# Turning the memory tiles in pairs between mixing units, and filling the last cross head from two output units instead of four

## What is computed

```python
x = x + merged @ w_mix_out[l]
x = x + cross_attention(rms_norm(x, xattn_norm_g[l]), rms_norm(mem, mem_norm_g[l]),
                        w_xq[l], w_xkv[l], w_xo[l])
x = x + swiglu(rms_norm(x, ffn_norm_g[l]), w_ffn_gate[l], w_ffn_up[l], w_ffn_down[l])
```

## Time and profile before

| | |
|---|---|
| device time, median of 3 runs | 2035.38 us (2035.09 to 2038.58) |
| device time of the profiled execution | 2037.93 us |
| its span, first to last instruction | 2036.1 us |
| mean granted clock of PE | 0.989 of full |
| PE busy | 1944.5 us, 95% |
| DVE, ACT, POOL busy | 1075.8, 496.6, 1240.7 us |
| DMA | 177.39 MB, 87 GB/s in the mean |

### The profile page before, as it was taken

One profiled execution on the slowest core, in us unless ns is written; L12 is line 12 of the kernel. 1 busy time (PEld: TensorE's weight loads), 2 busy tenths in 40 slices (PEclk: granted clock), 3 DMA queues, 4 the chain that ended last, 5 costly groups with the idle time before them and its releaser, 6 DMA issues.

```text
span 2036.1 us, 23483 instructions
## 1 busy us (share of the span) xinstructions
PE 1944.5 (95%) x9015; PEld 1594.0 (78%) x9015; DVE 1075.8 (53%) x1514; ACT 496.6 (24%) x998; POOL 1240.7 (61%) x1018
## 2 busy tenths in 40 slices
PE   8888887999999999999999999999999989999997
PEld 6666666888888888888888778888779878888886
DVE  5677758998364131227866675333655563223134
ACT  4444443432122010012233333100222221001012
POOL 6333326878766776676633444776667587676662
PEclk9999998999999999999999999999999999999999
DMA  5221102333333333333312322333433233333321
GB/s 161 72 60 56 53 25 78 99 107 104 95 94 96 101 93 94 102 94 94 92 46 59 78 63 69 98 93 88 124 94 105 72 104 95 102 94 95 102 78 57
DMA packets 341169, 177.39 MB, mean 87 GB/s; under 512 B 14453, under 2 KB 338203, under 8 KB 341060
## 3 DMA queue, kind: packets, MB, share of 16 engines
q1 hardware_dynamic: 338834, 173.14, 29.5%
q10 hardware_dynamic: 2226, 2.76, 0.6%
HBM read 173.75 MB, written 2.13 MB: 86 GB/s over the span
## 4 chain that ended last, share of the span: by engine, by line
PE 75%; DVE 18%; issue 3%; ACT 3%; POOL 0%; ACTq 0%; DMA 0%; SPq 0%; DVEq 0%; POOLq 0%
PE bank L650 22%; PE bank L654 22%; PE bank L652 22%; PE bank L772 2%; PE bank L749 1%; DVE aPR L1710 1%; DVE aPR L1712 1%; DVE IT L1818 1%; DVE XC L1799 1%; DVE HS L1828 1%; DVE HS L1829 1%; DVE aPR L1702 1%; PE bank L738 1%; PE bank L718 1%; DVE ACC L1823 1%
## 5 line engine op out<-in xcount | busy, mean ns | idle before, releaser
L615 POOL TENSOR_TENSOR WL<-RAW,WH 128x1024 fp32r<-128x1024 f32 (+3 forms) x331 | 812.9, 2456 | 27.5
L650 PE MATMUL bank<-HH,WH 128*128 128x512 f32 x1560 | 622.7, 399 | 14.6 <-DVE SQ L1670 7.4
L654 PE MATMUL bank<-HH,WL 128*128 128x512 f32 x1560 | 617.1, 396 | 0.0
L652 PE MATMUL bank<-HL,WH 128*128 128x512 f32 x1560 | 614.3, 394 | 0.0
L611 POOL TENSOR_TENSOR gate<-gate 128x1 f32<-128x1 f32 x331 | 89.2, 270 | 737.8 <-PE bank L654 687.9
L650 PEld LDWEIGHTS bank<-HH,WH 128*128 128x128 f32 x1560 | 295.3, 189 | 79.0 <-issue 20.6
L612 POOL TENSOR_SCALAR WH<-RAW 128x1024 fp32r<-128x1024 f32 (+3 forms) x331 | 344.6, 1041 | 0.0
L652 PEld LDWEIGHTS bank<-HL,WH 128*128 128x128 f32 x1560 | 295.4, 189 | 60.1 <-issue 4.2
L654 PEld LDWEIGHTS bank<-HH,WL 128*128 128x128 f32 x1560 | 294.7, 189 | 60.4 <-issue 1.9
L1869 DVE TENSOR_TENSOR X<-X,bank 128x512 f32<-128x512 f32 x80 | 54.9, 687 | 202.7 <-PE bank L654 202.7
L650 PE MATMUL bank<-UH,WH 128*128 128x512 f32 x256 | 99.9, 390 | 0.3
(11 more groups left out here) (407 smaller groups left out, 3205.0 us busy)
## 6 DMA issues: line engine op xcount, KB each, us to landing
RAW<-in_w_in SPq DMA_DIRECT2D x107, 512.0 KB, 3.7
RAW<-in_w_up SPq DMA_DIRECT2D x32, 512.0 KB, 3.9
RAW<-in_w_down SPq DMA_DIRECT2D x32, 512.0 KB, 3.9
RAW<-in_w_ffn_gate SPq DMA_DIRECT2D x22, 512.0 KB, 3.7
RAW<-in_w_ffn_up SPq DMA_DIRECT2D x22, 512.0 KB, 3.7
RAW<-in_w_xkv SPq DMA_DIRECT2D x16, 512.0 KB, 3.8
RAW<-in_w_ffn_down SPq DMA_DIRECT2D x16, 512.0 KB, 3.5
RAW<-in_w_proj_attn SPq DMA_DIRECT2D x8, 512.0 KB, 3.8
```

The lines of the kernel that those rows point to most:

```text
L615: nc.gpsimd.tensor_tensor(WL[:, s, 0:k, :], RAW[:, s, 0:k, :], WH[:, s, 0:k, :].bitcast(F32), ALU.subtract).then_inc(S_[f"unit_cut{s}"], 1)
L650: mm(psum[s][:, 0:n], WH[:, s, k, :], hi(k), start=(k == 0), stop=False)
L652: mm(psum[s][:, 0:n], WH[:, s, k, :], lo(k), start=False, stop=False)
L654: last = mm(psum[s][:, 0:n], WL[:, s, k, :], hi(k), start=False, stop=(k == tiles - 1))
```

## The change

It rewrites where the pairs of transposes stand: tiles 2e−8 and 2e−7 both behind unit e, for e from 4 to 7; nothing stands inside a unit or in the queries. `mem_after` is changed to match, so that ACT and DVE handle the same two tiles behind the norm chunk of unit e. In the last cross head the fronts are those of two output units, 36 matmuls instead of 72; the fills are 4, 4, 4, 12 and 6, 6 instead of 6, 6, 6, 18 and 10, 12, so 36 instead of 58 issue inside the head, and none of the fronts behind it. Units 2 and 3 of the output then run whole behind the tails of units 0 and 1.

```diff
--- before.py
+++ after.py
@@ -408,7 +408,7 @@
 
         def mem_after(e):
 
-            return {4: [0], 5: [1, 2], 6: [3, 4], 7: [5, 6, 7]}.get(e, [])
+            return [] if e < 4 else [2 * e - 8, 2 * e - 7]
 
         KIND1, KIND_FOX, KIND_SWA = Causal(1), Causal(2), Window(2)
         block = top.enter_context(nc.Block())
@@ -1007,18 +1007,11 @@
                 last.then_inc(S_["mem_t"], 1)
 
             for e in range(DC):
-                rows = from_pair("out2", e // 4, e % 4, MGC, cut_pair("mgc_hi", "mgc_lo") if e == 0 else None)
-                if e >= 5:
-                    run(rows, 12)
-                    mem_transposed(2 * e - 9)
-                run(rows)
-                if e >= 4:
-                    mem_transposed(2 * e - 8)
-
-            queries0 = from_h("cross", 0, 0, cut_of("n4"))
-            run(queries0, 12)
-            mem_transposed(DC - 1)
-            run(queries0)
+                run(from_pair("out2", e // 4, e % 4, MGC, cut_pair("mgc_hi", "mgc_lo") if e == 0 else None))
+                for m in mem_after(e):
+                    mem_transposed(m)
+
+            run(from_h("cross", 0, 0, cut_of("n4")))
             norm_stat("n4", "n3")
             pe.wait_ge(S_["mem_acc"], DC + 1)
             mm(OUTB[:, 0:MEM], ones[:], ACCM[:], start=True, stop=True).then_inc(once("mem_stat")[0], 1)
@@ -1088,7 +1081,7 @@
                 cross(h, ahead, (8, 8, 8, 24), (16, 16))
                 run(ahead)
 
-            fronts = [from_pair("xout", 0, e, XO, cut_pair("x_out_hi", "x_out_lo", 2)) for e in range(4)]
+            fronts = [from_pair("xout", 0, e, XO, cut_pair("x_out_hi", "x_out_lo", 2)) for e in range(2)]
 
             def front_rows():
                 for rows in fronts:
@@ -1097,12 +1090,12 @@
                         yield
 
             ahead = front_rows()
-            cross(3, ahead, (6, 6, 6, 18), (10, 12))
+            cross(3, ahead, (4, 4, 4, 12), (6, 6))
             run(ahead)
             for rows in fronts:
                 run(rows)
-            for e in range(4, DC):
-                run(from_pair("xout", 1, e % 4, XO))
+            for e in range(2, DC):
+                run(from_pair("xout", e // 4, e % 4, XO))
 
 
             def ffn_group(name, g, first=False):
```

## The result

The changed kernel takes 2022.92 us in the median of 4 runs (2022.19 to 2023.13); the kernel before, with the run made beside it, 2036.98 (4 runs, 2035.09 to 2041.70). The ratio is 0.9924, with a 95% interval of 0.9906 to 0.9943: faster, by 12 to 19 us. The forecast was 2018.0, with a range from 2016.5 in its own case up to 2024. The range holds the result; the forecast itself is 4.9 us too low.

A forecast was written before the change was run, and what follows sets the result against it. TensorE, busy 95% of the span, was taken as the bound, so only its waits and low-clock work counted. Savings of 10.7 and 6.7 us, 17.4 off the 2035.38 median, gave 2018.0; range 2016.5 to 2024.

The forecast's parts named there:

- its own case: Whole kernel, forecast 2018.0, chance 0.52; fewer waits in the edited stages give 2016.5, run spread up to 2019.5.
- Part 1: Mixing units 4 to 7 and queries: transposes in double pairs take 25.90 us to the statistics against 36.59, −10.7 us.
- The breakdown by terms: Mixing stage's saving: some 7.6 us gaps, 4.9 low clock, 0.5 turns, with 2.5 given back.
- The port's rival: Mixing: POOL's WL starts ahead of tile 1's sum, later pairs wait, queries end 2.1 us later: 2020.1; chance 0.18.
- Part 2: Last cross head and output units: two fronts finish product 0 earlier, DVE's norm no longer binds, −6.7 us.
- (a): Last cross head, before the turns: PE waits 0.47 us for the last probabilities; bounds none and 1.8 us.
- The bound "none": Before the last head's turns: no wait if a DVE scaling that POOL holds up slips in ahead.
- (b): Before the last two rows of product 0: PE waits for XOL's first half, a gap of 1.57 us.
- The sum: Both edited stages together: 17.4 us less, from the profiled 2037.93 to 2020.5, from the median to 2018.0.
- the term of 4.9 us for the low clock: Mixing stage: PE's slow matmuls behind the waits at the memory tiles' transposes go, saving 4.9 us.

The follow-up runs named there:

- late sum: Changed kernel plus one 128x256 memset on VectorE ahead of tile 1's sum, delaying that sum; 2024.36 us, ratio 0.9936.
- the third of the same kernel: Changed kernel unedited, run a third time beside the kernel before; 2026.87 us, ratio 0.9936, profiled span 2018.5.
- both covers: Changed kernel with tiles turned spread over units 1 to 7 and 7 matmuls of output unit 2 put behind the last head; 2020.89 us, ratio 0.9913.

## Why the prediction was right, and where it was off

**Part 1** was forecast at 25.90 us and took 25.98. Its waits, as gaps in issue: tile 2, 0.31 forecast, 1463.78 − 1457.59 − 0.42 − 5.44 = 0.33 found; tile 3, 1.20 and 1.20; tiles 4 and 5 none and none; tile 7, 0.95 and 1477.81 − 1476.80 − 0.14 = 0.87. The turn of two pairs at 0.42 holds. So does the clock, 1.00 in the whole stretch. (The breakdown by terms in the prediction, 7.6 + 4.9 + 0.5 − 2.5, gives 10.5 and not 10.7; the sum that the forecast goes by is the one of 25.90.) The port's rival (0.1 us of margin) did not come about, but it was real: shifted by 0.33, the sum sat out all of WL. Its price was over-stated, 1.6 instead of 2.1. So DVE and POOL meet not only at semaphores, as the opening section has it. The Trainium skill (SBUF — State Buffer, SBUF: two separate sides) says that whoever starts first keeps the ports for a whole instruction. The late sum (ended 0.28 behind WL) and the one of 0.90 (0.27 behind WH) agree with it; of the other order, a sum that holds up WL, the traces show only the 0.08 us above.

**Part 2** was forecast at −6.7 and gave −6.9 (73.14 to 66.23); against the other two profiles with four fronts it is 6.6 and 6.0. Of its two lost covers (a) was taken at 0.47 and cost nothing. The bound "none" was the right one, and for the reason named with it: with the earlier scores one scaling of the probabilities (at 1594.30) ran ahead of POOL's WL (from 1594.47). The next one (1595.34) was held up in its place, but took 1.72 where the one held up before took 2.26, and the last probabilities were ready 8.44 us behind the head's first scores instead of 9.30. From the scores to the first turn are 8.86 us, which is 11.61 less 12 matmuls. (b) was 1.57 and is 1607.03 − 1605.13 − 0.23 = 1.67. DVE no longer binds at two fronts, with 0.23 us to spare where 0.26 was forecast. In the later experiments it bound at three, by an idle of 1.64 where 1.7 was expected, and one front opened (a), by 1.74 where 2.3 was expected.

**The sum** was 17.4 for the two stages. Measured it is 10.6 + 6.9 = 17.5, and the spans of two traces whose start was equally early, 2036.1 and 2018.5, differ by 17.6.

**What failed** is the last step, "from the median the same difference gives 2018.0", in two ways. First the base: three runs had a median of 2035.38, but all 36 executions of the kernel before that were made lie at 2035.1 to 2043.5 with a median of 2039.1. The stated spread of 3.5 was taken as noise around the right middle. In fact two of the three lie at the very low end. Whether that was chance is not shown: the 36 were made in batches on several chips, and the medians of the later batches are 2039.3, 2037.5 and 2039.2. The base accounts for 3.7 of the 4.9 us. The 14 executions of the changed kernel lie at 2020.3 to 2028.4, median 2022.9, 16.1 below. Secondly, the term of 4.9 us for the low clock was counted as certain, since all three waits of one trace had it. In one of three profiles with these waits a wait left the clock alone, so the part is worth somewhat less than 10.6 in the mean: eight falls of nine, by these profiles, some 0.5 us less. What is left of the 4.9 us stays open. One sum of the range is off too: no wait at (a) and half of part 1's waits of 2.46 gone are 0.47 + 1.23, which gives 2016.3 and not 2016.5, and with half of (b) 2015.5.

In the profiles kept, the spread does not come from the edited stages. Those of the same text repeat within 0.2 us, apart from that one clock fall and from the slow matmuls behind the last head of four fronts ("to ff" 72.2 to 73.1). It comes from the last idle, and from the first 395 us, which the change does not touch. A scan on VectorE near 394 us, here in the profile after, begins anywhere from 393.4 to 399.7 us in the thirteen profiles, and from it to the mixing start are 1033.5 to 1034.2 us in all of them:

```profile
394.84 2.10 DVE L1821 TENSOR_TENSOR_SCAN HS<-RT,TT 128x512 f32<-128x512 f32 x1
```

The lower clock is not all of it. The same row of VectorE in the profile after and in the one with the late sum:

```profile
35.16 0.75 DVE L1672 SCALAR_TENSOR_TENSOR aQN<-aQN,PARAM,aRQ 128x512 f32<-128x512 f32 x1 [0.80 <-ACT aRQ L1158]
```

```profile
38.32 0.75 DVE L1672 SCALAR_TENSOR_TENSOR aQN<-aQN,PARAM,aRQ 128x512 f32<-128x512 f32 x1 [0.80 <-ACT aRQ L1158]
```

They are 3.2 us apart, and the granted clock of the first 35 us is 1.00 in both. Nor does the clock of a single stretch tell the start. From 300 to 350 us in the profile after, in the third of the same kernel, and in the one with both covers (columns as in the earlier trace rows):

```profile
300.00:350.00 50.00, 38.63 (x153) 30.87 (x152) 40.65 (x34) 17.84 (x23) 31.19 (x27) 0.83 0.24 69
```

```profile
300.00:350.00 50.00, 38.64 (x158) 31.01 (x157) 41.72 (x36) 19.13 (x25) 32.62 (x27) 0.90 0.24 69
```

```profile
300.00:350.00 50.00, 38.63 (x154) 30.91 (x153) 40.72 (x34) 19.01 (x25) 32.46 (x27) 0.83 0.24 69
```

Both clocks went with an early start: 1427.1 with 0.90, 1427.6 with 0.83 in the last, against 1428.7 with 0.83 in the first.

## What to carry to other kernels

Where a transpose waits for a helper engine, two behind a full product can be better than one in the middle: the helpers get the product's whole length. One behind each of more products was better still here, by 2.2 us. And when a norm's chain decides behind a stage, finish the first product early, even with less cover inside the stage, until the chain is paced by the products; beyond that point less cover only costs. Work such an edit out on intervals inside the trace. Give the whole time a base from many runs: here the stages were right to 0.2 us in the profile after, and the absolute time was off by 5.

## What the runs showed that was not expected

TensorE's clock did not fall after every idle of the same length: an idle of 2.32 us was followed by matmuls at full clock and one of 2.42 in the same profile by matmuls at half; 2.94 us ahead of the last statistics left them at 0.95 us or at 1.71 in two profiles of one kernel. In the three profiles with the old order of the pairs eight of nine such idles (2.22 to 2.46 us) were followed by slow matmuls. Over the twelve profiles behind the first the start of the untouched mixing stage lay anywhere from 1427.1 to 1433.5 us. Its differences are all there by 395 us and in part by 35 us, where the clock was still full in twelve of the thirteen; what sets them stays open. So does what made four of the 14 executions of the changed kernel take 2026.9 us and more, as none of them was profiled.
